# Feed-forward products of a diffusion trunk on one core: seven half-size products in place of eight

## What is computed

```python
def conv_glu(h, row_len, w_up, ffn_conv_w, w_down):
    u, gt = jnp.split(h @ w_up, 2, axis=-1)
    gt = grid_conv3x3(gt, ffn_conv_w, row_len)
    return (jax.nn.gelu(gt) * u) @ w_down
...
    x = x + gate2 * conv_glu(h, row_len, w_up, ffn_conv_w, w_down)
```

## Time and profile before

| | us |
|---|---|
| median of three executions | 1568.11 (1565.01 to 1570.07) |
| the profiled execution's own time | 1563.74 |
| its span in the profile | 1561.8 |
| PE busy | 1510.4 (97%) |
| DVE (VectorE) busy | 925.5 (59%) |
| ACT (ScalarE) busy | 482.2 (31%) |
| POOL (GpSimd) busy | 400.4 (26%) |

### The profile page before, as it was taken

How to read it: one execution, slowest core, us unless ns; L and a number is a source line. 1 busy time by engine, 2 the same in 40 slices (tenths; PEclk the granted TensorE clock), 3 DMA queues, 4 the chain that set the end, 5 groups by cost and what they waited for, 6 DMA issues and landing times.

```text
span 1561.8 us, 24209 instructions
## 1 busy us (share of the span) xinstructions
PE 1510.4 (97%) x9814; PEld 1466.1 (94%) x9814; DVE 925.5 (59%) x1402; ACT 482.2 (31%) x904; POOL 400.4 (26%) x204
## 2 busy tenths in 40 slices
PE   4999999999999999999999999999999999999997
PEld 2889999999989989998999999999999999999996
DVE  4652462669997894239864367336734673476257
ACT  5322343221267784234221222022102220221024
POOL 0011112550224452310421133123212222232120
PEclk9999999999999999999999999999999999999999
DMA  9735123532434566110111111111111111111103
GB/s 329 284 146 203 43 97 115 182 108 73 142 127 135 188 199 250 46 37 28 41 41 41 42 41 41 41 45 52 41 41 42 41 41 41 42 41 47 36 1 121
DMA packets 80257, 142.62 MB, mean 91 GB/s; under 512 B 19212, under 2 KB 52564, under 8 KB 78484
## 3 DMA queue, kind: packets, MB, share of 16 engines
q1 hardware_dynamic: 76260, 131.38, 25.1%
...
q0 software_dynamic: 432, 1.77, 0.3%
...
## 4 chain that ended last, share of the span: by engine, by line
PE 90%; DVE 4%; ACT 2%; DMA 2%; issue 1%; POOL 0%; SPq 0%; DVEq 0%; ACTq 0%; POOLq 0%
PE ps L2466 52%; PE ps L2468 26%; PE ps L1221 5%; PE ps L2395 1%; PE ps L2691 1%; PE ps L1194 1%; DVE fa L2287 1%; DMA araw<-wts 1%; PE ps L2592 1%; DMA X<-xT 0%; PE ps L2551 0%; PE ps L2445 0%; DVE ss L1907 0%; PE ps L2429 0%; PE ps L1166 0%
## 5 line engine op out<-in xcount | busy, mean ns | idle before, releaser
L2466 PE MATMUL ps<-hH,wH 128*128 128x384 f32 x1680 | 568.1, 338 | 5.6 <-issue 3.2
L2468 PE MATMUL ps<-hL,wH 128*128 128x384 f32 x1680 | 562.7, 335 | 0.0
L1347 POOL TENSOR_TENSOR wL<-raw,wH 128x1024 fp32r<-128x1024 f32 x93 | 226.3, 2433 | 880.5 <-ACT wH L1550 880.0
L2466 PE MATMUL ps<-hH,wL 128*128 128x384 f32 x1680 | 382.1, 335 | 0.0
L2466 PEld LDWEIGHTS ps<-hH,wH 128*128 128x128 f32 x1680 | 316.5, 188 | 15.1 <-issue 11.2
L1550 ACT ACTIVATE wH<-raw 128x1024 fp32r<-128x1024 f32 x99 | 105.0, 1061 | 724.8 <-PE ps L2466 724.8
L2468 PEld LDWEIGHTS ps<-hL,wH 128*128 128x128 f32 x1680 | 316.4, 188 | 0.0
L2287 DVE SCALAR_TENSOR_TENSOR fa<-G,cst,fa 128x1024 f32<-128x1024 f32 x176 | 296.5, 1685 | 15.4 <-DVE fa L2284 0.6
L2466 PEld LDWEIGHTS ps<-hH,wL 128*128 128x128 f32 x1680 | 299.8, 188 | 0.0
L2466 PE MATMUL ps<-pH,wH 128*128 128x384 f32 x528 | 179.5, 340 | 4.0 <-DVE pL L2311 1.8
L2174 DVE SCALAR_TENSOR_TENSOR X<-ps,mod,X 128x384 f32<-128x384 f32 x138 | 70.5, 566 | 188.8 <-PE ps L2466 188.8
...
## 6 DMA issues: line engine op xcount, KB each, us to landing
raw<-wts SPq DMA_DIRECT2D x103, 512.0 KB, 3.3
araw<-wts SPq DMA_DIRECT2D x48, 512.0 KB, 6.2
...
kv<-tok_d SPq DMA_DIRECT2D x16, 512.0 KB, 5.4
...
```

The source lines that it names most:

```text
L1347: nc.gpsimd.tensor_tensor(weight(1, u4), raw[:, u4 % RAW, :], weight(0, u4).bitcast(F32), ALU.subtract).then_inc(s["wl_ready"], 1)
L2466: last = M(out, lhs, rh[:, c], start=(k == 0 and not lo), stop=(lo and k == kts - 1))
L2468: M(out, lhs, rl[:, c], start=False, stop=False)
```

## The change

A product of a 2 x 2 arrangement of blocks by another normally takes eight block products; Strassen's scheme takes seven, of sums and differences of blocks. The change uses it for nearly all of the feed-forward part:

- **Up.** Four units are still multiplied as before (gates 0, 1, 2 and u 0). The other 40 are taken in pairs, a gate and a u block, in 20 steps. The halves of the weights are the two units by inputs 0 to 511 and 512 to 1023; those of the tokens are 0 to 575 and 576 to 1151. A step is seven products of 24 matmuls on 288 columns (4 input blocks, three terms, two column groups).
- **Weight forms.** For each product a form of 128 x 512 is needed: three of them lie in raw, four are sums (S1 to S4) that GpSimd makes (sum_1 to sum_4). ScalarE rounds each form, GpSimd subtracts to make its low part, both into rings of four.
- **Input forms.** Four differences of h by half (T1 to T4) are made once by VectorE, out of the sum hH + hL that GpSimd writes over X; X itself goes to memory and comes back later.
- **Outputs.** ScalarE copies four partial results of each step out of PSUM; VectorE adds or multiplies three of the four output quarters out of PSUM (c12, c11, c21), GpSimd does the fourth from copies (c22). fa gets three buffers; each finished p goes to memory.
- **Down.** After all of the up matrix come 10 steps in five chunks of four feed-forward blocks. p is read back by halves; VectorE makes four differences and three low parts, GpSimd four low parts (chunk_low), and VectorE adds each of 14 results per step to X (add). The tail of two blocks is multiplied as before.

The diff, cut to its core (lines of waits and of tile places are left out where nothing rests on them):

```diff
+UP_STEPS, DOWN_STEPS, FORMS = 20, 10, 7
+STEPS = UP_STEPS + DOWN_STEPS
+HT = T // 2
+HN = HT // 2
...
-    fa = place("fa", [P, 2, T], F32, blk(32) + ((GS + ZC) * 4 + 31) // 32 * 32)
+    fa = place("fa", [P, 3, T], F32, blk(32) + ((GS + ZC) * 4 + 31) // 32 * 32)
...
+            def h_part(i):
+
+                b, cols = NORM2[i]
+                pool.wait_ge(s["hL_ready"], KT + i + 1)
+                lo, hi = cols[0][0], cols[-1][1]
+                gp.tensor_tensor(X[:, b, lo:hi], hH[b][:, lo:hi].bitcast(F32), hL[b][:, lo:hi].bitcast(F32),
+                                 ALU.add).then_inc(s["h_ready"], 1)
+
+            after(pool, "x_out", 16 * KT)
+            for i in range(len(NORM2)):
+                h_part(i)
+                if i == 4:
+                    low(U_FFN + 2, U_FFN + 2)
+            low(U_FFN + 3, U_FFN + 3)
+
...
+            def form_low(i):
+
+                m, j = divmod(i, FORMS)
+                pool.wait_ge(s["wh_ready"], S0 + i + 1)
+                gp.tensor_tensor(grouped(m, ring(wL, i)), form_source(m, j), grouped(m, ring(wH, i)).bitcast(F32),
+                                 ALU.subtract).then_inc(s["wl_ready"], 1)
+
+            def sum_1(m):
+
+                for k in range(2):
+                    pool.wait_ge(raw_in[raw_slot(m) + k], raw_count(m, k))
+                if m:
+                    pool.wait_ge(s["wl_ready"], S0 + FORMS * (m - 1) + S4 + 1)
+                gp.tensor_tensor(grouped(m, sumQ[0][:, :]), quarter(m, 1, 0), quarter(m, 1, 1), ALU.add).then_inc(s["wsum"], 1)
...
+            def sum_3(m):
+
+                after(pool, "wsum", 4 * m + 3)
+                pool.wait_ge(s["wl_ready"], S0 + FORMS * m + S2 + 1)
+                gp.tensor_tensor(grouped(m, sumQ[1][:, :]), quarter(m, 0, 0), quarter(m, 1, 0),
+                                 ALU.subtract).then_inc(s["wsum"], 1)
...
+            def c22(m):
+
+                f = gate_of(m)
+                after(pool, "copied", 4 * m + 4)
+                gp.tensor_tensor(copy_u3[:], copy_u3[:], copy_p5[:], ALU.add).then_inc(s["p22_done"], 1)
+                after(pool, "p22_done", 2 * m + 1)
+                pool.wait_ge(s["gelu_done"], f + 1)
+                gp.tensor_tensor(fa[:, f % 3, HT:T], fa[:, f % 3, HT:T], copy_u3[:], ALU.mult).then_inc(s["p22_done"], 1)
+
+            def chunk_low(c, name):
+
+                read = {"T1": 2, "T2": 4, "T3": 3, "T4": 4}[name]
+                input_low(4 + 7 * c + PARTS.index(name) + 1, 4 + 4 * c + read, fl[c % 2][name][:],
+                          fs[c % 2][name][:], fh[c % 2][name][:])
+
+            after(pool, "h_ready", len(NORM2))
...
+            for m in range(1, STEPS - 1):
+                c = (m - UP_STEPS) // 2 + 1
+                ahead = m > UP_STEPS and m % 2 and c < GROUPS
+                form_low(FORMS * m + S3)
+                if m == UP_STEPS:
+                    chunk_low(0, "T3")
+                if ahead:
+                    chunk_low(c, "T1")
+                form_low(FORMS * m + A12)
+                if ahead:
+                    chunk_low(c, "T2")
+                sum_1(m + 1)
+                sum_2(m + 1)
+                form_low(FORMS * m + A22)
+                if m == UP_STEPS:
+                    chunk_low(0, "T4")
+                if ahead:
+                    chunk_low(c, "T3")
+                form_low(FORMS * (m + 1) + A11)
+                form_low(FORMS * (m + 1) + S1)
+                if ahead:
+                    chunk_low(c, "T4")
+                if m < UP_STEPS:
+                    c22(m)
+                if m == UP_STEPS - 1:
+                    chunk_low(0, "T1")
+                form_low(FORMS * (m + 1) + S2)
+                sum_4(m + 1)
+                if m == UP_STEPS - 1:
+                    chunk_low(0, "T2")
+                sum_3(m + 1)
+                form_low(FORMS * (m + 1) + S4)
...
+            def gate_in(f):
+
+                act.wait_ge(s["fc_done"], f)
+                if f < 3:
+                    act.wait_ge(side_free[0], (B_FFN + 1) // 2 + f)
+                else:
+                    after(act, "out_done", 3 * (f - 3) + 2)
+                A(gs[:, 1:ROWS + 1, 1:GRID + 1], fa[:, f % 3, 0:LAT].rearrange("p (r c) -> p r c", c=GRID), ACT.Copy)
+                A(gc[:, 1:CTX + 1], fa[:, f % 3, LAT:T], ACT.Copy).then_inc(s["gt_in"], 1)
...
+            def form_high(i):
+
+                m, j = divmod(i, FORMS)
+                if i >= 4:
+                    after(act, "prod_done", products(i - 3))
+                else:
+                    act.wait_ge(s["blk_done"], S0 if i > 1 else U_FFN + 1)
+                if j in (S1, S2, S3, S4):
+                    after(act, "wsum", 4 * m + (S1, S2, S4, S3).index(j) + 1)
+                else:
+                    for k in ((0, 1) if m >= UP_STEPS else (int(j == A22), )):
+                        act.wait_ge(raw_in[raw_slot(m) + k], raw_count(m, k))
+                A(grouped(m, ring(wH, i)), form_source(m, j), ACT.Copy).then_inc(s["wh_ready"], 1)
...
+            CONV_END = {0: {P2: 1}, 1: {P7: 2}, 2: {P6: 3}, 3: {P5: 4}, 4: {P1: 5, P2: 6}, UP_STEPS - 1: {P3: FB - 1}}
+            for m in range(UP_STEPS):
+                for p in range(FORMS):
+                    if p in (P1, P5, P6, P7):
+                        copy_out(m, p, {P1: copy_x, P5: copy_p5, P6: copy_u2, P7: copy_u3}[p])
+                    else:
+                        after(act, "prod_done", FORMS * m + p + 1)
+                    if m == 0 and p == P1:
+                        form_high(S4)
+                    form_high(FORMS * m + p + 4)
+                    f = CONV_END.get(m, {P2: m + 2}).get(p)
+                    if f is not None:
+                        gelu(f)
+                        if f < FB - 1:
+                            gate_in(f + 1)
...
+            V.tensor_tensor(T1s[:], X[:, 0:4, HT:T], X[:, 0:4, 0:HT], ALU.subtract).then_inc(s["form_sum"], 1)
+            V.tensor_tensor(T3s[:], X[:, 4:8, HT:T], X[:, 0:4, HT:T], ALU.subtract).then_inc(s["form_sum"], 1)
+            after(dve, "form_sum", 2)
+            V.tensor_tensor(T2s[:], X[:, 4:8, HT:T], T1s[:], ALU.subtract).then_inc(s["form_sum"], 1)
+            after(dve, "form_sum", 3)
+            V.tensor_tensor(T4s, X[:, 4:8, 0:HT], T2s[:], ALU.subtract).then_inc(s["form_sum"], 1)
...
+            def c21(m):
+
+                f = gate_of(m)
+                dve.wait_ge(s["gelu_done"], f + 1)
+                after(dve, "prod_done", FORMS * m + P4 + 1)
+                k = 2 * up_bank(m, P4)
+                V.tensor_tensor(two(fa[:, f % 3, 0:HT]), two(fa[:, f % 3, 0:HT]), ps[:, k:k + 2, 0:HN],
+                                ALU.mult).then_inc(s["out_done"], 1)
...
+            conv9(0)
+            conv9(1, {1: (first_up, 0), 6: (c12, 0)})
+            c11(0)
+            conv9(2, {1: (c21, 0), 7: (c12, 1)})
+            conv9(3, {2: (c11, 1), 4: (c21, 1)})
+            conv9(4, {1: (c12, 2), 5: (c11, 2), 7: (c21, 2)})
+            conv9(5, {4: (c12, 3), 7: (c11, 3)})
+            for f in range(6, FB - 1):
+                conv9(f, {1: (c21, f - 3), 7: (c12, f - 2)})
+                c11(f - 2)
+            conv9(FB - 1, {1: (c21, UP_STEPS - 2), 7: (lambda c: part_sum(c, "T1"), 0)})
...
+                k = 2 * down_bank(m, p, q)
+                gate = lambda which: mod[:, 40 + ob, which:which + 1]
+                if not second:
+                    last = V.scalar_tensor_tensor(two(X[:, ob, 0:HT]), ps[:, k:k + 2, 0:HN], gate(0), two(X[:, ob, 0:HT]),
+                                                  ALU.mult, ALU.add)
+                else:
+                    for lo, hi, b, at, which in ((HT, HT + HN, k, 0, 0), (HT + HN, LAT, k + 1, 0, 0),
+                                                 (LAT, T, k + 1, LAT - HT - HN, 1)):
+                        last = V.scalar_tensor_tensor(X[:, ob, lo:hi], ps[:, b, at:at + hi - lo], gate(which),
+                                                      X[:, ob, lo:hi], ALU.mult, ALU.add)
+                last.then_inc(s["out_done"], 1)
...
+            def product(bank, lhs, kbs, right, fresh):
+
+                for kb in range(kbs):
+                    rh, rl = right(kb)
+                    for w, lo in ((wH, False), (wL, True)):
+                        for n in range(2):
+                            out, c = ps[:, 2 * bank + n, 0:HN], slice(n * HN, n * HN + HN)
+                            last = M(out, lhs(w, kb), rh[:, c], start=(fresh and kb == 0 and not lo),
+                                     stop=(lo and kb == kbs - 1), skip_group_check=not fresh)
+                            if not lo:
+                                M(out, lhs(w, kb), rl[:, c], start=False, stop=False, skip_group_check=not fresh)
+                last.then_inc(s["prod_done"], 1)
...
+            for m in range(UP_STEPS):
+                for p in range(FORMS):
+                    i = FORMS * m + p
+                    pe.wait_ge(s["wl_ready"], S0 + i + 1)
```

(16 more changed lines are left out.)

576 lines of the change are left out of this document (407 added, 169 removed).

## The result

| | us |
|---|---|
| the kernel before, median of four executions | 1566.63 (1565.01 to 1570.07) |
| the changed kernel, median of four | 1611.11 (1608.97 to 1612.75) |
| ratio, with its 95% interval | 1.0286 (1.026 to 1.0312) |
| forecast | 1609 (1516 to 1665) |
| the profiled execution of the changed kernel | 1608.97, its span 1607.1 |

What follows compares the result with a forecast made beforehand. The old kernel was taken as bound by PE's streamed columns, the new up part by alternating VectorE and GpSimd turns. Up end 1324 + 7 + 224 + 5 + 43 = 1603 us span, 1605 with surroundings, 1609 as median; range 1516 to 1665.

Steps and rivals of the forecast that it cites:

- The bound of 173.4: PE's matmuls on 288 columns: upper limit of 173.4 ns each, meaning no gain below 384 columns.
- the rival that rested on it: PE: 288 columns cost what 384 do, PE sets both parts, end near 1714 us; chance 0.05.
- 11.9 + 13.8 = 25.7 us of turns: Up step: VectorE's taps (11.9) and 13 GpSimd instructions (13.8) exclude one another, so their sum is the shortest step.
- the lower bound: Up step: 24.1 us if each of the 13 GpSimd instructions holds VectorE off for only about 0.93 us.
- The working beside it: Up step by an exclusive lock for the whole recorded GpSimd instruction: about 27 us, the sum 25 us higher.
- PE sets the step after all: Up step: GpSimd's instructions slip into DVE's gaps, 22.4 us a step, 1518 as a median; chance 0.18.
- Waiting on wL: Up part, sign of being right: PE busy for some 85%, its waits being for GpSimd's low parts of weights.
- The 85% for PE: Up part, sign of being right: PE busy for some 85%, POOL for nearly all of it.
- reading A: Raised after the profile, not in the prediction: ScalarE's place waiting for a convolution, with copies queued behind, sets the up step.
- 7 at the change from up to down: Change-over: 7 us, as the first chunk's preparation (18.9 us of turns) falls beside the last convolution, only half covered.
- this rival: Up part: PE loses its clock in the waits, 1.2 GHz in a quarter of steps, 73 us more, 1682; chance 0.05.
- DMAs at nothing: Whole sum: DMAs add no time, a step adding 0.6 MB of p to 1 MB of weights, some 60 GB/s.

Runs made afterwards that it cites:

- x1: Changed kernel plus one GpSimd subtraction of 512 columns, result unread, in each of 17 up steps: ratio 1.0435, convolutions finally 26.3 us apart.
- x3: Changed kernel with GpSimd's four weight sums cut from 512 to 16 columns in 19 up steps (wrong weights): 23.5 us a step, ratio 1.0070.
- x6: Changed kernel with the four sums, low parts of S1 to S4 and c22 moved to VectorE in up steps 4 to 18: 23.4 us, ratio 1.0155.
- x7: x6 with GpSimd's last three low parts (A11, A12, A22) also on VectorE in steps 4 to 18: 22.1 us a step, ratio 1.0013.
- x12: Changed kernel, start alone altered: nine of eleven sums over X by ScalarE, the input forms' four low parts by VectorE: ratio 1.0142.
- x10: Changed kernel with ScalarE's gelu of the last convolution, in the last up step, moved behind the copy of P7: ratio 1.0286.

## Why the prediction was right, and where it was not

**PE's own work.** Matmuls on 288 columns stand 132 ns apart as the median, against 133.4 taken; 288 x 1 / 2.4 GHz with the 13.4 ns by which 384 columns exceeded their own was the right scale. The 122.5 ns by the Trainium skill (TensorE: Matmul & The Clock Gate, Back-to-back issue gap), whose formula is that of an isolated matmul, are not reached in any run here; the lowest is 130. The bound of 173.4, and the rival that rested on it, are out.

**The up step.** 11.9 + 13.8 = 25.7 us of turns were forecast, 25.7 + 0.5 taken with idle moments; 25.1 were measured, 2% under the sum. The idle allowance was about right: GpSimd waits 0.4 us a step. What was too dear are the turns, 24.7 us in place of 25.7: a tap beside GpSimd is lengthened by 0.92 us (2.20 against 1.28) and not by 1.04, close to the 0.93 of the lower bound. The working beside it, at the recorded 2.40 us per 1024 columns, was added up wrongly: 6784 columns are then 15.9 us, the step 27.8 and not 27, and the sum some 42 us higher and not 25; the measured step is far below it, because the recorded time of a GpSimd instruction is longer than the time for which it holds VectorE off. x1 (an added turn costs its time), x3 and x6 (removed turns give time back) and x7 (with none left TensorE sets the step) show the mechanism.

**The rival of TensorE.** "PE sets the step after all" needed GpSimd's instructions to slip into VectorE's gaps. They don't, but the rival's own step of 22.4 us was nearly met where GpSimd's turns were removed: 22.1 in x7.

**What PE waits for.** "Waiting on wL" was wrong. The floor is set by the turns, but PE meets the loop at copy_x and c11; in the steady part it met GpSimd's wL only in x1, with GpSimd overfull, and in the changed kernel only for 2.9 us in the first steps and 6.4 in the down part. The prediction had named waits on ScalarE in place of wL as a sign of being wrong; x1, x3, x6 and x7 show that the sign was badly chosen and the floor was right. The 85% for PE were 90 in the middle and 85 over the up part (478.80 of 562).

**The start.** The norm was to end at 745 and ended at 746.36; 762 were forecast for the first convolution, which began at 758.6. x12 takes some 22 us of turns out of the start, by the prediction's prices, and gained 26, so these terms had the right size. What was missed is the order: P1 began at 774.0, a single gap of 15.7 us followed behind P5, and the first five steps took 41.8, 26.7, 34.4, 29.6 and 27.0 us. The gap hangs on ScalarE, though the profile names no releaser: by the program P6 needs the copy of P1 out of PSUM. ScalarE sat for 15.9 us at the end of the first convolution, that copy began only at 795.52, and PE went on at 796.25:

```profile
791.88 1.06 ACT L2087 ACTIVATE G<-fa 128x1024 f32<-128x1024 f32 x1 [15.89 <-DVE fa L2677]
...
795.52 0.63 ACT L2131 ACTIVATE copy_x<-ps 128x576 f32<-128x576 f32 x1
```

```profile
796.25 0.58 PE L3191 MATMUL ps<-T2h,wH 128*128 128x288 f32 x1 [15.73 <-issue]
```

So in the first step the place at which ScalarE waits (reading A) does cost PE time. How the rest of the five steps divides between VectorE's backlog and the low clock there (0.91 up to 1000 us) was not separated.

**The change-over.** This is the term that was mis-sized. "7 at the change from up to down, ... only half covered" measured 11.7 + 11.0 = 23 us (36.8 against 25.1, 34.0 against 23.0). It hardly showed in the sum because the lighter step, 14 times 0.6 to 1.1, gave it back: P1 of the down part was due at 1331 by the working and began at 1323.2.

**Down and tail.** From P1 on 229 us were forecast (224 + 5), 240.9 measured with the slow first step in it; the other nine average 23.0 where 22.9 were taken. The tail was 43.0 against 43. Sum: 1323.2 + 240.9 + 43.0 = 1607.1 of span against 1603. That the total fell within 2 us of the forecast is luck by so much as these errors cancel.

**Clock.** In the middle of the up part the granted clock stayed at 1.00, with waits of up to 1.6 us in every step, so that this rival does not set the step. But over the whole up part it was 0.95, again what the prediction had named as a sign of being wrong: it fell six times between 784 and 922 us and three times after 1312, each time with a wait of PE of 1.9 to 15.7 us. By stretches of 2 us PE was busy for some 37 us at the lower level of 1.2 GHz, so that an estimate of what this can have cost is 18 us at most; the sum had nothing for it. In the steady steps it cost nothing that shows: in x1 the clock was 0.93 between 962 and 1062 us and 0.97 from 1063 to 1300, and the convolutions stood evenly, 25.1 and then 26.3 us apart.

**DMAs at nothing.** Right in the steady part (65 GB/s, and no wait for raw among PE's, ScalarE's and GpSimd's there). At the change-over they carry 411 GB/s between 1305 and 1318 us, at a share of 1.03, and x10 shows one wait of 3.7 us of ScalarE for fs0B; whether that costs time is open.
